# Norm shift and scale before the transpose instead of after it, in a two-layer diffusion backbone with experts (one core, fp32)

## The reference, cut to what matters

```
mod = silu(c) @ w_mod[l] + b_mod[l]            # c of the latent tokens, c_ctx of the context tokens
shift1, scale1, gate1, shift2, scale2, gate2 = split(mod, 6)
h = rms_norm(x, g_norm1) * (1 + scale1) + shift1
x = x + gate1 * token_mixing(h)                # four attention mixers, gated, w_out
h = rms_norm(x, g_norm2) * (1 + scale2) + shift2
aff = softmax(h @ w_router)                    # 16 experts
gate, idx = top_k(aff.T, 2 * tokens / 16)      # 64 latent and 16 context rows per expert
y = (silu(h[idx] @ w_g) * (h[idx] @ w_u)) @ w_d
x = x + gate2 * scatter_add(y * gate)
```

## Time and profile before

| | us |
|---|---|
| median of 3 runs | 3149.83 (3146.45 to 3152.20) |
| the profiled execution: its own time | 3149.15 |
| its span, from first to last instruction | 3147.3 |
| PE busy | 2746.4 (87%) |
| DVE busy | 1984.2 (63%) |
| ACT busy | 1599.6 (51%) |
| POOL busy | 862.2 (27%) |
| weights and the rest read from HBM | 560.47 MB, mean 186 GB/s |

### The profile page before, as it was taken

The page is one execution under the profiler, slowest core; times in us unless marked ns, Lnnn a source line. Parts: engine busy times, 40 slices in busy tenths (PEclk is TensorE's granted clock), DMA queues, the critical chain, the costliest instruction groups (busy, mean ns, idle before and its releaser), DMA issues.

```text
span 3147.3 us, 41275 instructions
## 1 busy us (share of the span) xinstructions
PE 2746.4 (87%) x13702; PEld 1965.2 (62%) x13702; DVE 1984.2 (63%) x3185; ACT 1599.6 (51%) x2382; POOL 862.2 (27%) x513
## 2 busy tenths in 40 slices
PE   6869999999985988998979999998998689898984
PEld 2357777777774555555548777776777455555552
DVE  7853366435355888888865346644435788888885
ACT  5644444334233666666654444434324466666663
POOL 0003000311301444444441100111121254444443
PEclk9989999999996999999989999999997799999997
DMA  9932111211332999999982201211123599999996
GB/s 325 328 116 69 45 35 34 74 34 61 120 126 101 322 329 329 332 328 326 328 309 69 70 31 34 66 43 61 63 97 121 201 334 328 333 329 331 332 332 221
DMA packets 193419, 587.46 MB, mean 187 GB/s; under 512 B 26888, under 2 KB 36934, under 8 KB 193286
## 3 DMA queue, kind: packets, MB, share of 16 engines
q1 hardware_dynamic: 176886, 529.77, 48.1%
q0 software_dynamic: 16336, 55.81, 6.1%
q10 hardware_dynamic: 64, 0.13, 0.0%
HBM read 560.47 MB, written 25.16 MB: 186 GB/s over the span
## 4 chain that ended last, share of the span: by engine, by line
PE 56%; DVE 16%; issue 10%; DMA 8%; ACT 7%; POOL 1%; SPq 1%; ACTq 0%; DVEq 0%; POOLq 0%
PE bank L445 15%; PE bank L447 14%; PE bank L446 14%; DMA ring<-in_w_e_up 7%; DVE low L1724 4%; PE bank L835 4%; ACT high L1013 4%; PE bank L807 4%; DVE low L1290 3%; PE bank L825 2%; ACT bank L1063 1%; DVE xeT_low L1295 1%; DVE att L1374 1%; POOL low L1893 1%; DVE st L1551 1%
## 5 line engine op out<-in xcount | busy, mean ns | idle before, releaser
L1013 ACT ACTIVATE high<-ring 128x1024 fp32r<-128x1024 f32 (+1 forms) x1012 | 1047.4, 1050 | 538.2 <-PE bank L447 370.8
L1724 DVE TENSOR_TENSOR low<-ring,high 128x1024 fp32r<-128x1024 f32 (+1 forms) x564 | 836.6, 1515 | 233.1 <-ACT high L1013 232.4
L1893 POOL TENSOR_TENSOR low<-ring,high 128x1024 fp32r<-128x1024 f32 (+1 forms) x194 | 510.6, 2632 | 693.7 <-ACT high L1013 693.7
L445 PE MATMUL bank<-high,hT_high 128*128 128x512 f32 (+2 forms) x1280 | 517.0, 404 | 30.6 <-ACT sigr L1086 13.7
L445 PE MATMUL bank<-high,xeT_high 128*80 128x512 f32 x1024 | 422.3, 412 | 109.8 <-DVE xeT_low L1295 62.2
L447 PE MATMUL bank<-high,hT_low 128*128 128x512 f32 (+2 forms) x1280 | 483.6, 378 | 0.0
L446 PE MATMUL bank<-low,hT_high 128*128 128x512 f32 (+2 forms) x1280 | 482.1, 377 | 0.0
L446 PE MATMUL bank<-low,xeT_high 128*80 128x512 f32 x1024 | 411.8, 402 | 0.0
L447 PE MATMUL bank<-high,xeT_low 128*80 128x512 f32 x1024 | 411.4, 402 | 0.0
L1290 DVE TENSOR_TENSOR low<-ring,high 128x1024 fp32r<-128x1024 f32 (+2 forms) x254 | 302.1, 1221 | 112.7 <-ACT high L1013 111.1
L1184 ACT ACTIVATE att<-bank,st 128x640 f32<-128x640 f32 (+3 forms) x200 | 136.5, 683 | 348.3 <-DVE st L1556 253.6
(11 more groups left out here) (240 smaller groups left out, 3503.8 us busy)
## 6 DMA issues: line engine op xcount, KB each, us to landing
ring<-in_w_e_down SPq DMA_DIRECT2D x260, 512.0 KB, 4.7
ring<-in_w_e_gate SPq DMA_DIRECT2D x256, 512.0 KB, 6.0
ring<-in_w_e_up SPq DMA_DIRECT2D x256, 512.0 KB, 7.2
ring<-in_w_mod SPq DMA_DIRECT2D x96, 512.0 KB, 6.0
ring<-in_w_gate SPq DMA_DIRECT2D x64, 512.0 KB, 3.8
ring<-in_w_in SPq DMA_DIRECT2D x24, 512.0 KB, 4.8
ring<-in_w_branch SPq DMA_DIRECT2D x16, 512.0 KB, 4.2
ring<-in_w_out SPq DMA_DIRECT2D x16, 512.0 KB, 4.7
```

What stands on the lines that cost most here:

```text
L445: nc.tensor.matmul(out, lhs[0], rhs_high, start=start, stop=False)
L1013: A(high[:, g % HIGH, :, 0:w], ring[:, g % RING, :, 0:w], ACT.Copy).then_inc(high_done, 1)
L1724: V.tensor_tensor(low[:, (g + HIGH) % RING, :, 0:w], ring[:, (g + HIGH) % RING, :, 0:w], high[:, g % HIGH, :, 0:w].bitcast(F32), ALU.subtr ...
L1893: G.tensor_tensor(low[:, g % RING, :, 0:w], ring[:, g % RING, :, 0:w], high[:, g % HIGH, :, 0:w].bitcast(F32), ALU.subtract).then_inc(low_ ...
```

## The change

Shift and scale are applied to the tokens before they are turned, so the vectors are needed as rows, spread over all partitions.

- Modulation: all twelve rounds end as the gate rounds did. The rounds of a scale multiply with the norm's gain row while they copy. Every row is stored to `mod_rows`, by ScalarE's queue, two rounds later, through two buffers of `modsum`. The column tiles (`modcol`, `amod`, `gn_col`) and SP's four loads of gains in columns are gone; ScalarE's queue loads the gain rows.
- Tokens of layer 0 are loaded at the start. Rows of gain and shift (`mod_in`: four broadcast loads of 512 KB for each norm and layer) come by POOL's queue: for norm 1 of layer 0 during the modulation, of layer 1 between the token loads, for norm 2 while `w_out` runs.
- Norms: ScalarE squares and sums the row (`rms`), and takes the root in the same place, with the mean and epsilon in its scale and bias. VectorE scales with rstd and the gain row, and adds the shift row. What is turned is h itself: ScalarE only makes the high part. `x_normed` holds h. In norm 2 low parts follow two tiles behind instead of one.
- Experts gather h ready-made: `rows_mod` is gone, ScalarE's high part waits for the transposes and moves from chunk 4 to 3, VectorE's low part from 5 to 4.
- Router: `w_router` (16 columns) is the stationary operand, h (128 columns) moves; ScalarE copies each tile's logits to SBUF and TensorE turns them.
- Some tiles change their place in SBUF (`vmla`, `ckvT`, `cqT`, `kvn_b`, `gate2_b`, `gfin_b`); the residual's product goes to its own `wo_tmp`.

```diff
+        gain_b, shift_b = [two(M, 1408), two(M, 0)], [two(oTr, 0), two(M, 2 * D)]
+        wo_tmp = oTr[:, 2048:2560]
...
-                for w, g in ((0, g_norm1), (1, g_norm2)):
-                    for l in range(L):
-                        sp.dma_start(gn_col[:, 2 * l + w, :], g[l].rearrange("(k p) -> p k", p=P)).then_inc(const_in, 16)
...
-                if q % 3 < 2:
-                    if MOD_COLS[q] >= 2:
-                        pe.wait_ge(mod_col, MOD_COLS[q] - 1)
-                    for b in range(KD):
-                        ins = mm(bank(4 + MOD_COLS[q] % 2, 2 * b, 2 * b + 2), modrow[:, q % 2, b * P:(b + 1) * P], pair_sum[:, :],
-                                 start=True, stop=True)
-                    ins.then_inc(mod_tr, 1)
-                else:
-                    if q >= 3:
-                        pe.wait_ge(sum_ready, q // 3)
-                    for h in range(2):
-                        ins = mm(bank(6 + h)[0:2, :], pair_sum[:, :], modrow[:, q % 2, h * NW:(h + 1) * NW], start=True, stop=True)
-                    ins.then_inc(mod_sum, 1)
+                if q >= 2:
+                    pe.wait_ge(sum_ready, q - 1)
+                for h in range(2):
+                    ins = mm(bank(4 + 2 * (q % 2) + h)[0:2, :], pair_sum[:, :], modrow[:, q % 2, h * NW:(h + 1) * NW], start=True, stop=True)
+                ins.then_inc(mod_sum, 1)
...
+                def turn_logits(m):
+
+                    pe.wait_ge(lgT_ev, T * l + m + 1)
+                    return tr(bank(4, NE * m, NE * (m + 1)), affT[:, m * P:(m + 1) * P], ident[0:NE, 0:NE])
...
                 for m in range(T):
+                    pe.wait_ge(norm_low, 2 * (T * q2 + m + 1))
+                    for k in range(KD):
+                        ins = three(bank(6 + m % 2, 0, P)[0:NE, :], [t[:, k, :] for t in w_r2], hT[0][:, k, m * P:(m + 1) * P],
+                                    hT[1][:, k, m * P:(m + 1) * P], k == 0, k == KD - 1)
+                    ins.then_inc(lgT_full, 1)
                     if m + 3 < T:
                         norm_turn(q2, m + 3, 0)
-                    pe.wait_ge(norm_low, 2 * (T * q2 + m + 1))
-                    for k in range(KD):
-                        ins = three(bank(6, NE * m, NE * (m + 1)), [t[:, k, m * P:(m + 1) * P] for t in hT],
-                                    w_r2[0][:, k, :], w_r2[1][:, k, :], k == 0, k == KD - 1)
-                ins.then_inc(lg_full, 1)
+                    if m:
+                        turn_logits(m - 1)
+                turn_logits(T - 1).then_inc(lg_full, 1)
...
+            def mod_store(q):
+
+                act.wait_ge(sum_ready, q + 1)
+                act.dma_start(mod_dram[q // 6][:, q % 6 * D:(q % 6 + 1) * D], modsum[:, q % 2, :]).then_inc(mod_out[q % 2], 16)
...
+                if q >= 2:
+                    mod_store(q - 2)
+                if q % 3 == 0 and q:
+                    gain_row_in(q + 1)
...
+                def rms(q, m):
+
                     t = T * q + m
-                    act.wait_ge(var_ready, t + 1)
-                    A(sd[:, m:m + 1], var[:, m:m + 1], ACT.Sqrt).then_inc(sd_ready, 1)
-
-                def modulate(q, m, banks):
+                    if q % 2:
+                        act.wait_ge(x_new, T * l + m + 1)
+                    else:
+                        act.wait_ge(x_in[m], 16 * (q + 1))
+                    if t:
+                        act.wait_ge(sd_ready, t)
+                    A(sq, xt_of(q)[:, m, :], ACT.Square, accum_out=ss[:, m:m + 1]).then_inc(sq_done, 1)
+                    act.wait_ge(sq_done, t + 1)
+                    A(sd[:, m:m + 1], ss[:, m:m + 1], ACT.Sqrt, bias=eps, scale=1.0 / D).then_inc(sd_ready, 1)
+
...
+                def norm_highs(q, m):
 
                     t = T * q + m
                     for half in range(2):
                         act.wait_ge(norm_tr, 2 * t + half + 1)
-                        b = banks + 2 * (m % 2) + half
-                        for k in range(4):
-                            kk = 4 * half + k
-                            ins = A(bank(b, k * P, (k + 1) * P), bank(b, k * P, (k + 1) * P), ACT.Identity,
-                                    bias=shift_col(l, q % 2, kk, m), scale=gain_col(l, q % 2, kk, m))
-                        ins.then_inc(mod_done, 1)
-                        act.wait_ge(mod_done, 2 * t + half + 1)
-                        high_part(hT[0][:, 4 * half:4 * half + 4, m * P:(m + 1) * P], bank(b), norm_high)
+                        high_part(hT[0][:, 4 * half:4 * half + 4, m * P:(m + 1) * P], bank(2 * (m % 2) + half), norm_high)
...
-                    modulate(q1, m, 0)
+                        rms(q1, m + 1)
+                    norm_highs(q1, m)
+                    if l == 0 and m == 0:
+                        for b in range(2):
+                            act.wait_ge(mod_out[b], 16 * 3 * L)
...
+                def logits_out(m):
+
+                    act.wait_ge(lgT_full, T * l + m + 1)
+                    A(affT[:, m * P:(m + 1) * P], bank(6 + m % 2, 0, P)[0:NE, :], ACT.Copy).then_inc(lgT_ev, 1)
+
+                for m in range(2):
+                    rms(q2, m)
                 for m in range(T):
-                    if m + 1 < T:
-                        std(q2, m + 1)
-                    modulate(q2, m, 0)
+                    if m + 2 < T:
+                        rms(q2, m + 2)
+                    norm_highs(q2, m)
+                    if m >= 3:
+                        logits_out(m - 3)
+                for m in range(2, T):
+                    logits_out(m)
...
-                def rows_high(b, mods):
+                def rows_high(b, turned):
                     for half in range(2):
-                        act.wait_ge(xe_mod, mods + (half + 1))
+                        act.wait_ge(xe_tr, turned + (half + 1))
...
-                        if j == 4 and not last:
+                        if j == 3 and not last:
...
+                dve.wait_ge(mod_sum, q + 1)
+                if q >= 2:
+                    dve.wait_ge(mod_out[q % 2], 16 * (q // 2))
+                if q % 3 == 1:
+                    dve.wait_ge(g_row_in, 16 * (q // 3 + 1))
+                for h in range(2):
+                    dst, src = modsum[:, q % 2, h * NW:(h + 1) * NW], bank(4 + 2 * (q % 2) + h)[0:2, :]
+                    if q % 3 == 1:
+                        ins = V.scalar_tensor_tensor(out=dst, in0=src, scalar=1.0, in1=g_row[:, h * NW:(h + 1) * NW], op0=ALU.add, op1=ALU.mult)
+                    else:
+                        ins = V.tensor_copy(dst, src)
+                ins.then_inc(sum_ready, 1)
...
-                then(V.tensor_tensor_reduce(sq, xt[:, m, :], xt[:, m, :], 1.0, 0.0, ALU.mult, ALU.add, ss[:, m:m + 1]))
-                V.tensor_scalar(var[:, m:m + 1], ss[:, m:m + 1], 1.0 / D, EPS, ALU.mult, ALU.add).then_inc(var_ready, 1)
...
-                    V.tensor_scalar(xn[:, m % 2, :], xt[:, m, :], rstd[:, m:m + 1], None, ALU.mult).then_inc(xn_ready, 1)
+                    g = 1 if m < TS else 0
+                    if m in (0, TS):
+                        dve.wait_ge(gain_in[1 - g], 32 * (q + 1))
+                    then(V.scalar_tensor_tensor(out=xn[:, m % 2, :], in0=xt[:, m, :], scalar=rstd[:, m:m + 1], in1=gain_b[q % 2][:, g, :],
+                                                op0=ALU.mult, op1=ALU.mult))
+                    V.tensor_tensor(xn[:, m % 2, :], xn[:, m % 2, :], shift_b[q % 2][:, g, :], ALU.add).then_inc(xn_ready, 1)
...
-                for m in range(T + 1):
+                for m in range(T + 2):
                     if m < T:
                         residual(1, m, chunk_no(l, CH_DENSE - 1))
                         stats(q2, m)
-                    if m >= 1:
-                        norm_lows(q2, m - 1, 0)
+                    if m >= 2:
+                        norm_lows(q2, m - 2, 0)
...
-                def rows_mod(b, turned, base):
-
-                    for half in range(2):
-                        dve.wait_ge(xe_tr, turned + (half + 1))
-                        ks = slice(4 * half, 4 * half + 4)
-                        views = []
-                        for g, c0, c1 in ((1, 0, CAP_S), (0, CAP_S, CAP)):
-                            def wide(t, o):
-                                return t[:, o:o + 2 * KD].rearrange("p (k g) -> p k g", g=2)[:, ks, g:g + 1].broadcast_to([P, 4, c1 - c0])
-                            views.append((bank(6 + half, 0, 4 * CAP).rearrange("p (k n) -> p k n", k=4)[:, :, c0:c1],
-                                          wide(amod, (l * 2 + 1) * KD * 2), wide(modcol, (l * 6 + 3) * KD * 2)))
-                        (s0, a0, h0), (s1, a1, h1) = views
-                        V.tensor_tensor(s0, s0, a0, ALU.mult)
-                        exp_then(V.tensor_tensor(s1, s1, a1, ALU.mult), base + (half + 1))
-                        V.tensor_tensor(s0, s0, h0, ALU.add)
-                        V.tensor_tensor(s1, s1, h1, ALU.add).then_inc(xe_mod, 1)
...
```

(21 more changed lines are left out.)

106 lines of the change are left out of this document (35 added, 71 removed).

## The result

The changed kernel takes 3039.39 us (median of 4 runs, 3025.66 to 3041.34) against 3149.10 (4 runs of the kernel before). The ratio is 0.9642, interval 0.9612 to 0.9672. The profiled execution of the changed kernel has a span of 3038.1 us, 109.2 less than before.

What follows compares the result with a forecast made beforehand. No engine was full throughout; in the experts TensorE waited 4.1 us each, chiefly for the next tokens' low part. The terms -48 - 4.4 + 12 - 6.5 + 0 - 1 - 3 = -51 gave 3098 us, range 3052 to 3140.

Steps and rivals of the forecast that it cites:

- 2.7 us an expert: Experts: upper bound of the gain, 1.9 us of TensorE's wait for tokens' low part plus 0.8 for VectorE's low part.
- rival B: Router: the new form runs at full rate, -13.5 us a layer, 3072 us in all; chance 0.2.
- Experts: Both layers' expert stages: 1.6 us gained an expert, between bounds 0 and 2.7, for 30 experts: -48 us.
- Router: Output projection, second norm and router: new form priced at 0.213 us a matmul, -0.5 us a layer, -1 in all.
- Modulation: 0 to 180 us: row copies +6, gains' loads -3, tokens' loads +6.3, gain and shift loads +3: +12, bounds -3 and 18.
- First norm of layer 0: First norm and D projection of layer 0: -6.5 us, bounds -10 and 0.
- last norm: Final norm: ScalarE squares while VectorE scales, 2.3 us a tile against 3.1: -3 us, bounds -6 and 0.
- First norm of layer 1: First norm of layer 1: extra loads and dearer instructions against 3 us saved: 0, bounds -4 and +4.
- First gathers: First expert of each layer: 2.2 us bare between gather and first matmul goes, -4.4 us in all.
- Attention: D projection to second half of w_out, two layers: forecast change 0.
- Rival C: Norms: Square and Sqrt need different activation tables, two loads a tile, 64 us over 25 tiles, 3162 us; chance 0.05.
- Rival D: Experts: the wait for POOL's low part grows into the gap, gain 0.8 us an expert, 3122 us; chance 0.15.

Runs made afterwards that it cites:

- e1: Changed kernel with the experts' eight VectorE instructions back (multiplying by one, adding zero) and high and low parts at their old chunks: 3136.3 us, ratio 0.9928.
- e2: Changed kernel with only the places moved back (high part at chunk 4, low part at 5), no eight instructions: 3065.1 us, ratio 0.9713.
- e3: Changed kernel with the eight VectorE instructions kept at chunk 2, high part at 3, low part at 4: 3109.6 us, ratio 0.9854.
- e5: Kernel before with half of every expert weight chunk loaded and read twice, same instructions: 3095.5 us, ratio 0.9821.
- e14: Changed kernel plus eight VectorE instructions an expert on unused SBUF columns, which no other engine waits for: 3185.7 us, ratio 1.0107.
- e6: Changed kernel with the router's old form (tile stationary, 16 columns moving, no logits copies or turning): 3053.4 us, ratio 0.9692.
- e8: Changed kernel with ScalarE's four weight parts put between the third and fourth copy of the logits: 3031.0 us, ratio 0.9618.
- e7: Changed kernel with four groups of 24 extra TensorE matmuls during the choice of tokens, results unused: 3038.8 us, one run.

## Why the prediction was wrong, step by step

By its own terms the prediction could have had the number: with 2.7 us an expert and the router of rival B it is 3098 - 33 - 26 = 3039, though the text wrote 3045 and the range ended at 3052. That this meets the measured 3039 is luck in part: the experts gave 19 us more than even that, modulation, attention and the first norm of layer 1 took 14 more, and the router and the first gathers gave 5 less.

**Experts: the size and part of the mechanism.** The prediction's bound from the engines was 2.7 us an expert; with half the transfers the experiments give 2.82. The step that failed is "Next in line is the weight transfer. 0.95 of a possible 1.03 leaves at most 3.1 us per expert ... I take 1.6". I set off 1.1 us against a limit that I read from a share, and put the top of the range at 2.7. Measured are 3.4 (e1 and the changed kernel, 40.16 and 36.77). What came on top of 2.82, 0.57, is there only with full transfers, and the clock may be part of it. In eight-microsecond windows of the kernel before, 1080 to 1560, six stand at 0.79, five to fifteen windows apart, and all others at 1.00; they lie where TensorE waits. One without the drop, and one with it:

```profile
1184.00:1192.00 8.00, 5.50 (x23) 3.38 (x24) 8.00 (x12) 4.73 (x5) 2.53 (x1) 1.00 0.93 343
1224.00:1232.00 8.00, 6.59 (x22) 4.12 (x23) 8.00 (x11) 4.70 (x6) 2.50 (x1) 0.79 0.85 312
```

That is 10.1 us of lost clock (0.21 of 8 us, six times) in 12 experts, at most 0.84 each. The changed kernel has no such window in the same 480 us, nor have e2, e3 and e5; e1 has five. That the waits bring the clock down is what the order of events suggests; no run forced it.

The mechanism was half right. I had one wait in mind, a high part that comes late, and counted VectorE's 2.2 us as harmless where it has room. e3 and e14 say that it has none to give away: at 82% busy, in a loop where it may run only as far ahead as ScalarE's four chunks allow, its work still costs. By e1 and e2 2.5 of the 3.4 us are the instructions and 0.88 the places. Why the engine's idle time can't be used (the short look-ahead, or being held up beside GpSimd) is argued, no run separates it.

**Router: rival B, held at 0.2, came true but for 1.6 us a layer.** The step that failed is "narrow operands in this format are in a slow way of working, whose cost per column of a moving 128 I bound by 0.053 (full rate) and 0.213 (four times). I take 0.213". The row was read at a granted clock of 0.50, and it was set beside the earlier trace rows, read at 1.00 (222.2 to 230.4 us). The kernel before, in the stretch of the earlier trace rows, then the changed kernel:

```profile
942.78:947.00 4.22, 4.22 (x22) 4.22 (x21) 1.44 (x3) 4.16 (x12) 0.00 (x0) 0.50 0.23 95
952.00:963.00 11.00, 11.00 (x53) 11.00 (x54) 0.57 (x1) 1.18 (x1) 2.73 (x1) 0.50 0.01 1
```

```profile
943.00:948.00 5.00, 4.01 (x57) 3.66 (x55) 3.48 (x5) 1.42 (x4) 1.06 (x2) 1.00 1.01 398
955.00:960.00 5.00, 5.00 (x67) 4.53 (x65) 0.15 (x1) 0.64 (x3) 0.00 (x0) 0.90 0.01 3
```

```profile
942.99 0.22 PE L448 MATMUL bank<-hT_low,w_r_high 128*16 128x128 f32 x1
943.04 0.22 PE L449 MATMUL bank<-hT_high,w_r_low 128*16 128x128 f32 x1
...
954.35 0.31 PE L448 MATMUL bank<-hT_low,w_r_high 128*16 128x128 f32 x1
954.45 0.31 PE L449 MATMUL bank<-hT_high,w_r_low 128*16 128x128 f32 x1
```

In the new form the step is 0.06 us at the upper level (943.04 less 942.99, and 1.7 us for the 24 of a tile) and 0.10 to 0.11 at the lower (954.35 to 954.45), and the router runs mostly at the upper: its first matmuls come right behind w_out's last and eight transposes (942.85 us), while in the kernel before TensorE stood from 929.9 to 933.5, the clock fell to 0.50 at 932.6 and stayed there, and the router began at 935.06. Rival B had -13.5 a layer; measured -11.9. By e6 some 7 of them come even with the old form, by the earlier norm and a first router tile at the upper clock; the forecast had the norm's 4 us eaten by the router and by ScalarE's order. The Trainium skill, TensorE: Matmul & The Clock Gate, section LDWEIGHTS, has a load take about its columns over 1.2 GHz, by which 128 columns are an estimated 0.107 us; e6 shows 0.11 at the upper clock, so the trace agrees there. What I had called "twice the rule's" was the clock.

**Modulation: right within its bounds.** +16.1 against +12. Both terms were there (first bias add +4.5 for a forecast of +3.3; rounds +1.1 us each for 0.8). The rounds of before are 13.1 us in the mean, not the 12.6 that the prediction gave. In e1 to e3 and e6 to e8, which leave the stage alone, the last bias add lies at 184.1 to 186.3, so +12 to +14 is as good a measure of it.

**First norm of layer 0, last norm: right.** -6.6 for -6.5, and -3.1 for -3. The last norm's tiles come 2.35 us apart (forecast 2.3), because of the two output buffers, as the third tile's wait says:

```profile
3019.18 1.29 DVE L1387 SCALAR_TENSOR_TENSOR att<-att,st,M 128x1024 f32<-128x1024 f32 x1
...
3022.30 1.28 DVE L1387 SCALAR_TENSOR_TENSOR att<-att,st,M 128x1024 f32<-128x1024 f32 x1 [1.59 <-DMA out<-att]
```

**First norm of layer 1:** +2.5 for 0, inside its bounds. **First gathers:** -2.2 for -4.4. In layer 0 the start of the transposes lies 4.1 us ahead of the first matmul before and 2.35 after, 1.7 for the forecast 2.2, since ScalarE's first high part had run beside VectorE's second half (995.00 of the kernel before). 0.7 us more between the exponential and the transposes take the rest; why, is open.

**Attention:** +7.8 us for 0, in code that the change doesn't touch. Its stretches show the clock, here 60 us of layer 0 of the kernel before and the same ones of the changed kernel:

```profile
350.00:410.00 60.00, 53.60 (x324) 42.32 (x323) 27.55 (x73) 26.11 (x55) 1.12 (x2) 0.97 0.14 40
```

```profile
359.50:419.50 60.00, 53.62 (x311) 42.12 (x310) 27.28 (x71) 26.22 (x55) 1.12 (x2) 0.94 0.14 40
```

0.03 of 60 us are 1.8 us; layer 0 has two such places more than before. In the kernels of the experiments the same stretch takes from 683.2 us (e3; as before) to 689.4 (e7), and in e5, whose attention is that of the kernel before, 687.1 and 686.0. So this line of the table is chance, and not of the change.

Rival C (other activation tables) is out: both kernels have 16 table loads, and in each of the five norms one stands between the first square and its root and none between the later ones. Rival D is seen in the matmuls' waits for GpSimd's low part, 13.6 us in 500 after the earlier trace rows had 12.1 in 560, 0.1 us more in an expert; the weight loads' waits for it grew as well, from 19.6 to 29.8 us in 1080 to 1540.

## What to carry to other kernels

Before two rows of TensorE are compared, read the granted clock of both: a step at 1.2 GHz looks like a slow form of an instruction. An engine that is busy 82% and feeds another through a short look-ahead may have no room, and work taken from it can count nearly in full; to know, add idle work and watch the period, and with it the granted clock and how long the engine's other instructions become. A DMA share near 1 says that the engines are occupied, not that they can't give more: 0.95 went with 330 GB/s and 0.99 with 360.

## What I had not expected of the hardware

VectorE's instructions between SBUF tiles can take the length of a GpSimd instruction that runs beside them: 128 x 256 in 0.41 or 2.49 us, 128 x 1024 low parts in 1.2 us alone and 1.5 us in the mean, while those that read PSUM held 0.42 to 0.43: in the kernel before all 22 of L1674's 128 x 256 ones in 1080 to 1540 ran beside a GpSimd low part and none took longer. Which resource the two share no run here shows.
